# Where a two-block transformer kernel issues its probabilities' round trips, and when it does two side tasks

## What is computed

```
h  = rms_norm(x, g_attn) * (1 + sc_a) + sh_a
hc = rms_norm(ctx, g_attn) * (1 + csc_a) + csh_a
p  = softmax(q @ k.T * scale + bias)         # per head, 256 queries x 512 keys
o  = p @ v
x  = x + gt_a * (concat(o) @ w_out)
x  = x + gt_f * swiglu(rms_norm(x, g_ffn) * (1 + sc_f) + sh_f, wg, wu, wd)
```

## Time and profile before

| | |
|---|---|
| median of 3 runs | 2415.64 us (2413.65 to 2415.98) |
| the profiled execution | 2418.69 us |
| its span, first to last instruction | 2416.9 us |
| PE busy | 2389.6 us, 99% |
| DVE busy | 1810.4 us, 75% |
| ACT busy | 1109.0 us, 46% |
| POOL busy | 147.4 us, 6% |
| granted TensorE clock, mean | 0.998 of 2.4 GHz |
| DMA | 565.38 MB, mean 234 GB/s |

### The profile page before, as it was taken

How to read it: one execution, slowest core, us unless ns; L and a number is a source line. 1 busy time by engine, 2 the same in 40 slices (tenths; PEclk the granted TensorE clock), 3 DMA queues, 4 the chain that set the end, 5 groups by cost and what they waited for, 6 DMA issues and landing times.

```text
span 2416.9 us, 28495 instructions
## 1 busy us (share of the span) xinstructions
PE 2389.6 (99%) x10980; PEld 1965.0 (81%) x10980; DVE 1810.4 (75%) x2441; ACT 1109.0 (46%) x1448; POOL 147.4 (6%) x211
## 2 busy tenths in 40 slices
PE   9999999999999999999999999999999999999998
PEld 7888888888888888888787878777888888888887
DVE  5688868888899888888978885677777755555555
ACT  5344444444445454456743342645544443444443
POOL 2000000000000000000012210011000000000000
PEclk9999999999999999999999999999999999999999
DMA  9888766666688668877987786355898976667773
GB/s 302 258 270 271 241 221 193 196 185 193 187 275 263 213 216 309 274 256 263 315 272 239 243 259 210 125 160 194 268 303 286 295 227 191 199 212 225 211 212 125
DMA packets 282821, 565.38 MB, mean 234 GB/s; under 512 B 19160, under 2 KB 24558, under 8 KB 281149
## 3 DMA queue, kind: packets, MB, share of 16 engines
q1 hardware_dynamic: 270588, 515.16, 66.7%
q0 software_dynamic: 11808, 46.31, 6.5%
q10 hardware_dynamic: 288, 2.10, 0.2%
HBM read 547.33 MB, written 19.31 MB: 234 GB/s over the span
## 4 chain that ended last, share of the span: by engine, by line
PE 88%; DVE 7%; DMA 2%; issue 2%; ACT 1%; POOL 0%; SPq 0%; ACTq 0%; POOLq 0%; DVEq 0%
PE pb L2202 86%; PE pb L2206 2%; DVE wlo L1430 2%; DMA raw<-in_w_in 2%; DVE acc L1453 2%; ACT whi L969 0%; DMA ctn<-in_ctx 0%; DVE turn_t L1920 0%; DVE sm L1902 0%; DVE sm L1993 0%; DVE x L1810 0%; POOL rs L692 0%; DVE hcl L1772 0%; DVE gn L2062 0%; DVE x L1813 0%
## 5 line engine op out<-in xcount | busy, mean ns | idle before, releaser
L969 ACT ACTIVATE whi<-raw 128x1024 fp32r<-128x1024 f32 (+1 forms) x791 | 828.1, 1049 | 1112.7 <-PE pb L2202 990.5
L1430 DVE TENSOR_TENSOR wlo<-raw,whi 128x1024 fp32r<-128x1024 f32 (+1 forms) x791 | 952.9, 1212 | 442.8 <-ACT whi L969 440.7
L2202 PE MATMUL pb<-whi,xh 128*128 128x512 f32 (+1 forms) x1184 | 465.0, 393 | 1.5 <-DVE xl L1584 1.1
L2202 PE MATMUL pb<-whi,xl 128*128 128x512 f32 (+1 forms) x1184 | 458.2, 387 | 0.0
L2202 PE MATMUL pb<-wlo,xh 128*128 128x512 f32 (+1 forms) x1184 | 457.6, 386 | 0.0
L1453 DVE SCALAR_TENSOR_TENSOR acc<-raw,silc,acc 128x512 f32<-128x512 f32 x480 | 346.8, 752 | 8.1 <-DMA raw<-in_w_ada 3.1
L2202 PE MATMUL pb<-whi,fh 128*128 128x512 f32 x704 | 274.7, 390 | 1.5 <-DVE fl L2050 1.4
L2202 PE MATMUL pb<-whi,fl 128*128 128x512 f32 x704 | 274.0, 389 | 0.0
L2202 PE MATMUL pb<-wlo,fh 128*128 128x512 f32 x704 | 273.9, 389 | 0.0
L2202 PEld LDWEIGHTS pb<-whi,xh 128*128 128x128 f32 x1184 | 222.5, 188 | 47.6 <-issue 2.9
L2202 PEld LDWEIGHTS pb<-whi,xl 128*128 128x128 f32 x1184 | 222.4, 188 | 46.0
(11 more groups left out here) (425 smaller groups left out, 2787.5 us busy)
## 6 DMA issues: line engine op xcount, KB each, us to landing
raw<-in_w_in SPq DMA_DIRECT2D x375, 512.0 KB, 4.7
raw<-in_w_ada SPq DMA_DIRECT2D x192, 512.0 KB, 5.2
raw<-in_ffn_wg SPq DMA_DIRECT2D x88, 512.0 KB, 4.5
raw<-in_ffn_wu SPq DMA_DIRECT2D x88, 512.0 KB, 5.1
raw<-in_ffn_wd SPq DMA_DIRECT2D x88, 512.0 KB, 4.1
raw<-in_w_branch SPq DMA_DIRECT2D x64, 512.0 KB, 3.8
raw<-in_w_out SPq DMA_DIRECT2D x64, 512.0 KB, 4.6
scr_h<-sil POOLq DMA_DIRECT2D x11, 512.0 KB, 4.1
```

Of the source, the lines that this page charges most:

```text
L969: return eng.activation(dst, src, ACT.Copy)
L1430: tt(wlo[:, u, a:b, 0:n], raw[:, l % NRAW, a:b, 0:n], f32(whi[:, u, a:b, 0:n]), ALU.subtract) \
L2202: return eng.matmul(dst, l, r, start=start, stop=stop)
```

## The change

Four things. (1) `probabilities` moves from POOL's queue to SP's. SP gets a beat count of its own: behind each wait for a free raw tile it advances to the beat in which DVE frees that tile, and the eight round trips run at turn_p and turn_p + 2 of that count (POOL: + 1 and + 3). (2) `pv` is turn_p + 8 instead of + 7, and head 3 of na starts one beat later. (3) The rates of modulation steps change. (4) The transposes of the latents and all that follows from them come three beats later.

```diff
-        ADA_RATE |= dict.fromkeys(("wo", "nkc", "nvc", "nq", "nk", "nv", "gq", "mlq"), 0.5)
-        ADA_RATE |= dict.fromkeys(("gkv",), 1.0)
-        ADA_RATE |= dict.fromkeys(("mlc", "dfk", "dfv"), 1.25)
+        ADA_RATE |= dict.fromkeys(("wo", "nkc", "nvc", "nq", "nk", "nv", "mlq"), 0.5)
+        ADA_RATE |= dict.fromkeys(("gq",), 0.25)
+        ADA_RATE |= dict.fromkeys(("gkv",), 0.75)
+        ADA_RATE |= dict.fromkeys(("mlc",), 1.25)
+        ADA_RATE |= dict.fromkeys(("dfk", "dfv"), 1.6)
         ADA_RATE |= dict.fromkeys(("dfq",), 0.75)
-        ADA_RATE |= dict.fromkeys(("p1", "p2", "p3", "o0", "o1"), 0.46)
+        ADA_RATE |= dict.fromkeys(("p1", "p2", "p3", "o0"), 0.46)
...
-        ADA_RATE |= dict.fromkeys(("p0", "o2", "o3", "fg0"), 0.0)
+        ADA_RATE |= dict.fromkeys(("p0", "o1", "o2", "o3", "fg0"), 0.0)
...
+        freed_at = {load_of[i]: b for b, v in split_at.items() for i in v}
+        freed_at |= {load_of[i]: 0 for i in range(LEAD)}
+        freed_at |= {l: i - LEAD for i, v in ada_at.items() for _, _, l in v}
...
-        B["na"] = [E["nv"] + 3 + 3 * h for h in range(3)] + [E["nv"] + 15]
+        B["na"] = [E["nv"] + 3 + 3 * h for h in range(3)] + [E["nv"] + 16]
...
-        B["pv"] = {k: b + 7 for k, b in B["turn_p"].items()}
+        B["pv"] = {k: b + 8 for k, b in B["turn_p"].items()}
...
+            def probabilities(c, h):
+                b = B["turn_p"][c, h]
+                yield from until(b)
+                W.wait_ge("turned", c, h, 1)
+                eng.dma_start(scr_p[c, h].rearrange("t p x -> p t x"), turn_t[h % 2][:, :, :]) \
+                    .then_inc(*M.inc(S(f"scr_p{h % 2}"), "scr_p", c, h, by=16))
+                yield from until(b + 2)
+                W.wait_ge("scr_p", c, h)
+                rows = scr_p[c, h].rearrange("t (i c) x -> c (t i) x", i=4)
+                for a in range(4):
+                    eng.dma_start(prob_t[c, h][32 * a:32 * a + 32, :, :, :].rearrange("p t k r -> p t (k r)"),
+                                  rows[:, :, 128 * a:128 * a + 128]) \
+                        .then_inc(*M.inc(S(f"prob_in{h % 2}"), "prob_t", c, h, a, by=16))
...
+            chains = [probabilities(c, h) for c in ("na", "gq") for h in range(4)]
             load_x(0)
             for l, (kind, s, a, c) in enumerate(loads):
                 if l >= NRAW:
                     W.wait_ge("raw_free", l - NRAW)
+                    while beat[0] < freed_at[l - NRAW]:
+                        beat[0] += 1
+                        for g in chains:
+                            next(g, None)
...
```

More of the change, by code:

```diff
@@ L635, in sp, with until @@
             W = Waits(eng, M, dry)
+            beat = [0]
             xv = I["x"][0].rearrange("(b p) d -> p b d", p=128)
+            def until(b):
+                while beat[0] < b:
+                    yield
+            def probabilities(c, h):
[11 more added lines that the diff above has]
+                        .then_inc(*M.inc(S(f"prob_in{h % 2}"), "prob_t", c, h, a, by=16))
             def load_x(c):
@@ L833, in na_bias @@
                             .then_inc(*M.inc(S(f"nab_in{n}"), "nab", h, r, by=16))
[L835 to L847, removed]
             def gqa():
@@ L949, in pool @@
                       ln_rows("ln_d", B["ln_d"], 3, "conv_ln_g", "conv_ln_b"), tables(), attention1(), residual(),
-                      context(), norm1(), gqa(), mla1(), out2(), gates(), norm2(), hidden(), final(), na_bias(), diff(),
-                      *[probabilities(c, h) for c in ("na", "gq") for h in range(4)]]
+                      context(), norm1(), gqa(), mla1(), out2(), gates(), norm2(), hidden(), final(), na_bias(), diff()]
             for i in range(NSUB + 2):
@@ L1232, in mla1 @@
                 for kp in range(2):
-                    yield from until(B["ml1"] + 6 + kp)
+                    yield from until(B["ml1"] + 9 + kp)
                     W.wait_ge("cqT", kp)
@@ L1240, in mla1 @@
                                        scale=pcol("mq", kt)).then_inc(*M.inc(S("mla_hi"), "cqh", kt))
-                yield from until(B["ml1"] + 8)
+                yield from until(B["ml1"] + 11)
                 W.wait_ge("ckT", 2)
@@ L2481, in mla1 @@
                 for kp in range(2):
-                    yield from until(B["ml1"] + 5 + kp)
-                    ps = take(("cqT", kp), ("cql", kp), B["ml1"] + 6 + kp)
+                    yield from until(B["ml1"] + 8 + kp)
+                    ps = take(("cqT", kp), ("cql", kp), B["ml1"] + 9 + kp)
                     W.wait_ge("mln", "q", 1)
@@ L2489, in mla1 @@
                     ins.then_inc(*M.inc(S("side"), "cqT", kp))
-                yield from until(B["ml1"] + 7)
+                yield from until(B["ml1"] + 10)
                 for kt in range(3):
-                    ps = take(("ckT", kt), ("ckl", kt) if kt < 2 else ("kpT",), B["ml1"] + 8)
+                    ps = take(("ckT", kt), ("ckl", kt) if kt < 2 else ("kpT",), B["ml1"] + 11)
                     W.wait_ge("mln", "c", 3)
```

## The result

The changed kernel takes 2418.43 us (median of 20 runs, 2416.38 to 2424.32) against 2415.8 for the kernel before on the same chips (20 runs, 2413.07 to 2417.64): ratio 1.0016, 95% interval 1.0009 to 1.0023. It is slightly slower, 4.4 us above the predicted range. The profiled execution took 2419.58, its span 2417.8.

The account below looks back on a forecast made before the run. PE's queue was taken as the path. Gains of 1.72 + 4.58 + 1.2 + 0.90 - 0.3 = 8.1 us off the 2415.64 median gave 2407.5 us; the 8-in-10 range was 2404 to 2414.

Parts of the forecast that it names:

- Part 2: Products with the values a beat later, window head 3 two: PE's 1.72 us wait for prob_t goes, no added work.
- Part 4: Latent transposes moved from dfq to dfk: 4.58 us of PE waits and 1.2 for the clock, less 0.3.
- 4.58: PE's three idle times before the ml_c transposes, 0.89 + 0.98 + 2.71 us, all expected to go.
- Part 3: Modulation loads moved between strips: gain 0.90 us at the start of o2, no cost in dfk and dfv.
- Cost 0: Six more loads in dfk and dfv, 9.0 us of DVE, were to fit in 13.5 us left there.
- Part 1: Round trips moved from POOL's queue to SP's: taken as 0 us, with 2.5 us of cost kept for the range.
- the four trips of my sum: Window head 3 and gq heads 1 to 3: SP held 2.0 us at the median landing, 8.2 at 9.5 us.
- POOL is off the path, worth 0: Freeing POOL's powers from standing behind a wait for a landing was to gain nothing.
- C: Rival: SP held between beats 451 and 472, weights starve PE; 2427.8 us, deciding from 13.8 us held; chance 0.08.
- D: Rival: nothing moves, trips begin later and eat their extra beat, idle times keep their size; 2415.6 us, chance 0.10.
- B: Rival: stall moves with the transposes, ACT held at 473 to 475, PE waits there; gain 2.6, 2413.0 us, chance 0.17.
- My sentence that PE is the path: PE busy 2389.6 of 2416.9 us, so only its idle time and slow stretches, 27.3 us, could be won.

Follow-up runs that it names:

- pv alone: Kernel before with latent transposes three beats later and every product with the values one beat later, window head 3 in place: 2415.36 us, ratio 1.0001.
- latents alone: Kernel before with only the latent transposes moved three beats later: 2412.26 us, ratio 0.9992.
- latents + o1's loads: Kernel before with latent transposes three beats later and two modulation loads moved from o1 to dfv: 2411.49 us, ratio 0.9983.

## Why the prediction was wrong

**Part 2, the step that failed.** "Gain 1.72"; one beat "is new cover". The wait for prob_t of the window head did go, in every version with the trips on SP or with later window products. But products and head 3 later cost 0.0016 in the change (1.0016 against 1.0000, 3.9 us). I counted the beat as free since PE's work was the same and never asked what DVE does while head 3 is not yet there: it waits, and everything behind it in its queue, the freeing of raw buffers included, comes 2.5 us later. Nor were the 1.72 us a stall of their own: in *pv alone*, without the later head, PE only goes on to gq_kv's bank and waits 3.0 us there. How the 3.9 us divide between the head and the products is not settled, since each half alone is within the noise.

**Part 4, right in mechanism, too large.** 5.5 us were expected; the strips mlc to dfk of the version with the latents alone are 6.0 us shorter in the trace (waits and clock), but the ratios give 2 us and the medians 3, and 2.7 inside the change (1.0027 less 1.0016); each of these is at the edge of the noise. So 4.58 is the term that was too large, while in that trace the clock did stay at 1.00. I took the waits of one profiled execution, itself 3 us above the median, off the median. A second profile of the same kernel had smaller ones.

**Part 3.** The gain at o2 was right in kind: o1 and o2 are 1.33 us shorter than in the first trace, for 0.90, and 0.6 shorter than in the second. "Cost 0" is not settled: a lean of 0.0011 against it with the latents, of 0.0012 for it inside the change. One error of reading is plain: DVE works a load off four beats ahead, so dfk's first loads fall in dfq's beats of 2.8 us, not in the long ones of dfk that I counted on.

**Part 1.** "0" is within the intervals with the latents (0.0003), not alone (0.0011, interval above 0). SP's waits for the landing of a write are

```profile
SPq L76 <- DMA scr_pgq<-turn_t: 3.9, 3, 2.0
SPq L76 <- DMA scr_pna<-turn_t: 3.7, 1, 3.7
```

The 3.7 us stand at window head 2 (until 1319.64), outside the four trips of my sum. In those four SP was held 3.9 us: not at window head 3, and 1.2, 0.8 and 2.0 at gq heads 1 to 3. I had 2.0 for the median landing and 8.2 for the longest. What I sized wrong is the two beats: SP came to the second wait 2.6 to 4.0 us after it had issued the write of these gq heads, not 7.0 to 9.6. It was not held longer since the writes landed sooner in SP's queue, min/median/max, than in the earlier trace rows:

```profile
DMA to landing us min/median/max: 3.0/3.8/7.0
```

The page "DMA: Bandwidth & Descriptors" of the Trainium skill, section "Queues, rings and completion order", says that each DMA engine takes turns between the queue rows that have work and takes up a ring's descriptors in order. The shorter landing agrees with a write that shares with no second queue; that this is the reason is not shown. But "POOL is off the path, worth 0" was wrong: with the trips on POOL inside the change, its held power is in the chain. And the 2.3 us of issues that I set at 0 are in the chain of the change.

**The rivals.** C fell: SP was held 3.9 us in its stretch, short of the 13.8 from which C decides, and PE waits for no wlo in mlc or dfq; only the one at o2 went (3.3 to 2.4 us). D fell: the old waits went. B had the right kind, a stall that moves along with ACT held by a tile at 475, and the wrong place and price. PE met it at the copies of df_q and, which no rival had, of ml_q at the other end of the stretch. The sum treated each idle time of PE as a thing to be removed. But behind the wait in mlc stood another, for ACT's copies, which PE met once the first was gone; in dfq and dfk the renamed waits point to the same. My sentence that PE is the path was the premise that failed, between 1323 and 1430 us.

**What stays open.** Why gq's later products cost and how df_q is made later than without products and head 3 (neither traced to a queue), and why trips and rates lean one way on the kernel before and the other in the change. Taking back latents, trips or rates makes the change 2.7, 1.7 and 2.9 us slower, taking back the products 3.9 faster; by these sums the change should gain 3.4, and it loses 3.9, a gap of 7.3. But only the last of the four is clear of the noise, and the intervals together allow some 7 us, about as much as the gap. So that the parts don't add, and that they stand in for each other at the same late tiles, agrees with the renamed waits, but is not shown by the times.

## What to carry to other kernels

Before a wait of the busiest engine is taken off, follow the chain of work behind it to where it leaves that engine: if several waits share the same late tile, count them once. An item put one beat later leaves the in-order queue that must work on it standing idle for it, and all that is behind it there comes later; so look at what else is in that queue. When the gains sought are of the size by which executions of one kernel differ, try each part alone and take each part back; here that left one part and a piece of another, and 4 us.

## What was not expected of the hardware

Of the raw tiles issued from 1400 to 1430, weights and modulation together, the median took 7.3 us to land, and 4.9 with half of the modulation loads' bytes (the weight tiles alone, still 512 KB, 7.7 and 5.3, five tiles each); halving 34 of 192 loads was worth 4.6 us on the kernel before, as much as the best edit of order (4.1). Four reads took 1.81 us to issue on SP and 2.29 to 2.48 on POOL. After the idle times of 3.0 and 4.9 us the granted clock of the window was 0.93; without the late products, with single waits of 0.8, 1.6 and 1.3 us, it was 1.00 in both windows. Idle time alone does not tell: at the same place, prob_t of window head 3, the window from 1350 to 1375 had 1.00 around a wait of 2.3 us (latents alone) and 0.93 around one of 2.4 (latents + o1's loads).
